# The low parts of the weights are written over the raw ones, panel loads wait for the end of a product, and x tiles are asked for ahead of the panel

## The reference

```
xn = rmsnorm(h, g_mix)
z, xbc, dt, q, k, v = split(xn @ w_in)               # w_in: 1024 x 2312
y_ssd = conv + SiLU + chunked state-space scan (8 heads x 64, state 128, chunks of 128)
y_att = sliding-window attention (8 heads, window 128, bias table, sinks)
h = h + concat(y_ssd, y_att) @ w_out                 # 1024 x 1024
h = h + cross_attention(rmsnorm(h), memory K/V)      # w_cq 1024 x 512, w_co 512 x 1024
h = h + (silu(hn @ w_gate) * (hn @ w_up)) @ w_down   # hn = rmsnorm(h); 1024 x 2816, 2816 x 1024
y = rmsnorm(h)
```

## Time and profile before

| | us |
|---|---|
| median of 3 runs | 3246.65 (3242.48 to 3249.24) |
| profiled execution, own time | 3245.05 |
| its span | 3243.3 |

### The profile page before, as it was taken

One profiled execution on the slowest core, in us unless ns is written; L12 is line 12 of the kernel. 1 busy time (PEld: TensorE's weight loads), 2 busy tenths in 40 slices (PEclk: granted clock), 3 DMA queues, 4 the chain that ended last, 5 costly groups with the idle time before them and its releaser, 6 DMA issues. The chain is left out here.

```text
span 3243.3 us, 35792 instructions
## 1 busy us (share of the span) xinstructions
PE 2996.9 (92%) x13972; PEld 2396.2 (74%) x13972; DVE 1484.3 (46%) x2221; ACT 1135.1 (35%) x1826; POOL 1027.3 (32%) x507
## 2 busy tenths in 40 slices
PE   7877999999999999999999999999779999667898
PEld 5656787877877878778778787788668888565742
DVE  5655655666346556553465566524352222313111
ACT  4542464345233543452346434422332222111100
POOL 3200433333444333334443333344224444410000
PEclk8988999999999999999999999999889999656679
DMA  4146423222335232223352222233313332571256
GB/s 132 53 116 155 136 72 89 71 72 79 98 107 166 72 88 72 72 79 97 107 167 78 85 72 66 85 97 114 107 40 97 98 98 91 152 210 45 64 183 222
DMA packets 490989, 332.44 MB, mean 103 GB/s; under 512 B 58559, under 2 KB 458051, under 8 KB 490806
## 3 DMA queue, kind: packets, MB, share of 16 engines
q1 hardware_dynamic: 486318, 323.74, 34.3%
q10 hardware_dynamic: 1880, 6.34, 0.5%
q0 software_dynamic: 2624, 0.09, 0.1%
HBM read 309.86 MB, written 21.23 MB: 102 GB/s over the span
## 5 line engine op out<-in xcount | busy, mean ns | idle before, releaser
L799 POOL TENSOR_TENSOR w_lo<-w_raw,w_hi 128x1024 fp32r<-128x1024 f32 x400 | 973.9, 2438 | 1717.6 <-ACT w_hi L813 1717.6
L1583 PE MATMUL L<-xa_h,w_hi 128*128 128x512 f32 x1536 | 613.2, 399 | 4.0 <-DVE xa_l L1402 4.0
L1584 PE MATMUL L<-xa_h,w_lo 128*128 128x512 f32 x1536 | 601.6, 392 | 0.0
L1585 PE MATMUL L<-xa_l,w_hi 128*128 128x512 f32 x1536 | 601.0, 391 | 0.0
L813 ACT ACTIVATE w_hi<-w_raw 128x1024 fp32r<-128x1024 f32 x400 | 421.1, 1053 | 437.6 <-PE L L1585 431.2
L1583 PEld LDWEIGHTS L<-xa_h,w_hi 128*128 128x128 f32 x1536 | 290.0, 189 | 75.1 <-issue 11.4
L1585 PEld LDWEIGHTS L<-xa_l,w_hi 128*128 128x128 f32 x1536 | 290.1, 189 | 61.6
L1584 PEld LDWEIGHTS L<-xa_h,w_lo 128*128 128x128 f32 x1536 | 290.4, 189 | 58.9 <-issue 1.0
L1542 DVE TENSOR_TENSOR sg<-sg,L 128x512 f32<-128x512 f32 x88 | 60.5, 688 | 531.4 <-PE L L1585 531.4
L1583 PE MATMUL L<-hid_h,w_hi 128*128 128x512 f32 x704 | 280.0, 398 | 6.1 <-DVE hT L1550 6.1
L1584 PE MATMUL L<-hid_h,w_lo 128*128 128x512 f32 x704 | 274.8, 390 | 0.0
(11 more groups left out here) (489 smaller groups left out, 4413.0 us busy)
## 6 DMA issues: line engine op xcount, KB each, us to landing
w_raw<-in_w_gate_dram SPq DMA_DIRECT2D x88, 512.0 KB, 3.8
w_raw<-in_w_up_dram SPq DMA_DIRECT2D x88, 512.0 KB, 3.8
w_raw<-in_w_down_dram SPq DMA_DIRECT2D x88, 512.0 KB, 3.4
w_raw<-in_w_in_dram SPq DMA_DIRECT2D x56, 512.0 KB, 3.8
xt<-xT_dram SPq DMA_DIRECT2D x48, 256.0 KB, 4.1
wS<-in_w_down_dram SPq DMA_DIRECT2D x11, 1024.0 KB, 4.9
wS<-in_w_gate_dram SPq DMA_DIRECT2D x10, 1024.0 KB, 5.1
wS<-in_w_up_dram SPq DMA_DIRECT2D x10, 1024.0 KB, 5.1
```

What stands on the lines that cost most here:

```text
L799: pool.tensor_tensor(w_lo[:, n % RING, 0:w], w_raw[:, n % RING, 0:w], w_hi[:, n % RING, 0:w].bitcast(F32), ALU.subtract)\
L1583: pe.matmul(acc, wh, rh, start=(k == 0), stop=False)
L1584: pe.matmul(acc, wl, rh, start=False, stop=False)
L1585: last = pe.matmul(acc, wh, rl, start=False, stop=(k == kn - 1))
```

## The change

- `w_lo` lies at the offset of `w_raw`: the subtraction writes its result over its own first input. The arena is 12288 bytes smaller, and all that lay behind the low parts moves down.
- Since the low part now lives in the raw place until its product has been made, `load_panel(n)` waits for `lin_out`, the end of product n-3, and no longer for its low part.
- x tiles: the first four of a block go ahead of panel w0+3, tile j four panels after the W step that uses tile j-4, and both tests are made before the panel's load (`x_before[t] <= n`), so that a tile is issued, and its wait stands, ahead of the load of that panel.
- In block 0 SP's transposition block stands at w0+3, as the waits of the other blocks do.

```diff
-            x_before.append(w0 + (5 if b == 0 else 4) if j < XR else min(w0 + use[j - XR][0] + 6, NPAN))
+            x_before.append(w0 + 3 if j < XR else min(w0 + use[j - XR][0] + 4, NPAN))
...
-        arena_bytes = 207232
+        arena_bytes = 207232 - 12288
...
-        O_H = 3 * RING * 4096
+        O_H = 2 * RING * 4096
...
-        w_lo = at("w_lo", O_LO, [P, RING, D], F32R)
+        w_lo = at("w_lo", O_RAW, [P, RING, D], F32R)
...
                 def load_panel(n):
                     if n >= RING:
-                        sp.wait_ge(s["lo_ready"], n - RING + 1)
+                        sp.wait_ge(s["lin_out"], first_out[n - RING + 1])
...
-                        if b == 0 and n == w0 + 4:
+                        if b == 0 and n == w0 + 3:
...
-                        if n == w0 + (4 if b == 0 else 3):
+                        if n == w0 + 3:
...
-                    load_panel(n)
-                    while t < len(x_tiles) and x_before[t] <= n + 1:
+                    while t < len(x_tiles) and x_before[t] <= n:
                         load_x_tile(t)
                         t += 1
+                    load_panel(n)
```

## The result

The changed kernel takes **3368.95 us**, median of 4 runs (3365.92 to 3373.53), against 3245.89 us of the kernel before beside it (4 runs): ratio 1.038, 95% interval 1.0362 to 1.0398. It is 123 us slower; 3335 was predicted, with a range of 3278 to 3385. The profiled execution took 3370.76 us, its span 3369.0 is 125.7 longer than the 3243.3 of before.

What follows compares the result with a forecast made beforehand. TensorE, busy 92% of the span, was taken as the bound. Terms 33.6 + 5.4 + 33.4 + 5.1 + 2.3 + 9 = 88.8 us on 3245.05 gave 3333.9, forecast as 3335; own range 3285 to 3378, 8 in 10 for 3278 to 3385.

Steps and rivals of the forecast that it cites:

- main case: Whole kernel: the listed costs sum to 88.8 us, giving 3335 us; chance 0.62.
- Down groups: First down panel of a group: ACT's landing wait and POOL delay hid_l and the eviction; 11 x 3.05 = 33.6 us.
- Groups with attention between products: The 9 other down groups in blocks 0 to 2: longer product slots cover part; 5.4 us.
- W: Output projection, blocks 1 to 3: y stores held behind SP's wait for a product, plus late x tiles; 33.4 us.
- Boundary: Block boundary, last down product: W's panel 1 lands later, squares wait, DVE recovers 1 us; 1.7 us three times, 5.1.
- W of block 0: Output projection of block 0, no y to store: high parts already at about T+5 behind ACT's own work; 0.
- K, Q and the input projection: K, Q and most of the input projection, all blocks: foretold at 0.
- O: Block 3's sums of squares before the O and Q ends meet a later POOL subtraction; 2.3 us.
- Clock: TensorE after idling may return at half rate: charged at a third of the 11 places and block 3's stall; 9 us.
- Hidden: Rival: weights keep 3.4 us of slack and landings are quick enough, so nothing changes, 3247 us; chance 0.06.
- Much slower: Rival: in attention stretches each pair of steps loses 1 to 1.3 us, some 18 pairs a block; 3390 us, chance 0.11.
- Faster: Rival: POOL's later subtraction frees DVE early in a product, and x tiles come early; some -12 us, 3235, chance 0.06.

Runs made afterwards that it cites:

- e2: Changed kernel with ACT making hid_h ahead of the next high part in a feed-forward step: 3306.36 us, 64 over the kernel before.
- e7: Kernel before with only the change's SP order (x tiles ahead of the panel, block 0's SP block a panel earlier): 3278.69 us, +34.
- e6: Kernel before with loads waiting for the end of the product three before, SP's block at block 0 a panel earlier: 3380.35 us, +138.
- e8: Changed kernel with four places in the ring instead of three: 3276.66 us, 32 over the kernel before.
- e9: e8 with the x tiles asked for behind the panel again, as late as in the kernel before: 3258.80 us, +17.
- e15: Kernel before with ACT's order alone: hid_h, and squares of outputs 0 and 1 of the last down group, ahead of the high part: 3245.05 us, +3.
- e3: Changed kernel with y chunks 0 and 1 stored ahead of load w0+6, and hid_h ahead of the next high part: 3287.71 us, +45.
- e5: e3 with block 1's row of norm factors loaded at chunk 7 of SP's block, not at its end: 3289.15 us, +45.
- e1: Changed kernel with y chunks 0 and 1 stored ahead of the load of W's panel w0+6: 3337.80 us, 95 over the kernel before.
- e4: e3 with squares of outputs 0 and 1 of the last down group made ahead of the next high part: 3272.76 us, +28.

## Why the prediction was right, and where it was not

The main case came: 123 us slower, 34 more than the sum, inside the range. The mechanisms were those foretold, and both large terms were right. That the whole lies in the range is in part luck: some 18 of the 34 us come from stretches that the sum had at 0, and the range reached so far for other reasons (a slow clock at every place, a dearer W).

- *Down groups.* 11 places at 3.05, 33.6 us. Measured, the 11 products come 2.92 to 3.76 us late, 33.6 in all, POOL's subtraction 0.47 us ahead of hid_l as in the earlier trace rows; e2 shows the cause.
- *Groups with attention between products.* 5.4 foretold, 6.9 measured, gone in e2.
- *W.* 33.4 against 32.6. The store goes 1.93 us after product w0+4 starts (1.95 foretold), but lands in 3.9 us (1010.01 to 1013.95), not 5.6 (which was given as the mean of 6.7 and 4.7; that is 5.7); that is made up by what follows, since products w0+6 and w0+7 come late too. What the sum did not have is that the x order would have made the store late by itself (e7); its 2 us for the x tiles was wrong in sign (e6).
- *Boundary, the term mis-sized:* 5.1, measured 12.9. I placed the late high part in the last product and let DVE recover. The one that costs is the product before: its first square waits behind the high part of W's first panel, DVE's copy behind that for POOL.
- *W of block 0, the step that failed:* 0, measured 5.9. The high part at about T+5 was taken to leave room for a later load and for x tiles ahead of it. Load w0+3, asked for at 321.50 and behind four x tiles, needed 11.7 us to land, the high part came at T+11.9 and TensorE idled 4.4 us. The x tiles ahead are not the whole of it, as e6 shows, where they stand behind: there that panel landed 5.7 us after its issue (320.01 to 325.69), but the first x tile, issued at 327.24, landed only at 330.7, ACT had its rounding ahead of the high part, and TensorE idled 4.7 us. With a load that waits for a product, one of the two is late. SP and ACT of the changed kernel, then DVE and ACT of e6:

```profile
321.50 3.89 SPq L662 DMA_DIRECT2D w_raw<-in_w_out_dram  x3
...
333.22 1.06 ACT L813 ACTIVATE w_hi<-w_raw 128x1024 fp32r<-128x1024 f32 x1 [4.81 <-DMA w_raw<-in_w_out_dram]
```

```profile
330.68 0.75 DVE L1131 SCALAR_TENSOR_TENSOR xt<-xt,pv,diag 128x512 f32<-128x512 f32 x1 [9.88 <-DMA xt<-xT_dram]
...
332.00 1.04 ACT L813 ACTIVATE w_hi<-w_raw 128x1024 fp32r<-128x1024 f32 x1
```

- *K, Q and the input projection, the largest miss:* 0, measured 12.1. TensorE's idle there grew by 5.6 us; the rest goes with the granted clock, 0.96 in blocks 1 and 2 where it was 0.97 and 1.00. With early loads (e7) or four places (e8, e9) the row is under 3; no experiment took it apart, so its cause stays open. *O:* 2.3, measured 5.8.
- *Clock, mis-sized:* 9, of which 6 at a third of the 11 places. Measured at 6 of the 11: the product behind the idle runs in part at 1.2 GHz and takes 7.0 to 8.5 us instead of 5.44, 13.7 us in all. The changed kernel in block 2 (busy by engine, granted clock, DMA share, GB/s), ahead of such an idle and behind it:

```profile
2186.00:2216.00 30.00, 30.00 (x134) 24.85 (x133) 7.30 (x6) 9.05 (x11) 12.37 (x6) 1.00 0.33 98
2219.30:2222.70 3.40, 3.40 (x8) 2.72 (x9) 0.43 (x1) 1.06 (x1) 1.48 (x1) 0.50 0.02 5
```

With the idle gone (e2) all of it came back: the rows are at 0.0. At the place of block 0 shown above, the same idle was followed by a product of nearly full speed (5.56 us); which places fall is not foretold by anything I found.

- *Rivals.* "Hidden" would have been right about the weights: e2 has the late landings and no stall in the feed-forward. "Much slower" did not come: its 18 pairs a block are the 6.9 us above. "Faster" had no trace.
- *POOL's hold on DVE.* In the sum it is priced for hid_l, which reads two SBUF tiles. That was half of it: a copy and a scaling with one tile as input are held too (L1142 2.15 us against 0.42 for the shortest; the scaling 2.60 in e15, L1411 there, against 0.47). The Trainium skill (SBUF — State Buffer, Practical consequences) names, beside two SBUF inputs, a two-port mode of VectorE that copies and `tensor_scalar` can enter; by that rule, the trace agrees. The held copy makes the boundary of the changed kernel, the held scaling (L1408, 2.59 us at 950.01) the 2.0 us of the kernel before.
- *The own range* was added up loosely: the named terms give some 3292 and 3376, not 3285 and 3378. Neither bears on the outcome.

## What to carry to other kernels

When a transfer is made later, look less at its own slack than at what stands behind the instruction that waits for it on each in-order engine: here 3.3 us later landings were harmless to the weights and cost 48 us through one rounding queued behind them, and that came back when the two changed places. A store or load that another engine waits for should not stand behind a wait for a product. Two edits can each be enough for the same stall; undoing one then shows too little, and doing each alone shows too much (22.6 and 47.5 us in W, 32.6 together).

## What the runs showed that I had not expected

The x order is good or bad by the loads' waiting: with early loads it costs 34 us, with late ones it saves some 15 (e6 against the change, in the medians and in W). From 316 to 322 us the DMA engines moved only 32 to 50 GB/s (0.62 to 0.96 busy in the changed kernel, e3 and e5), with and without the broadcast load, and the kernel before has this stretch too. x tiles landed in 11 to 15 us there, where the median of all is 3.4. A stretch that no edit touches can differ by some 4 us between two executions: up to W of block 0, e1, e3 and e4 have the same code and took 2.8, 0.6 and -1.0 us more than the kernel before. So nothing is argued here from a single stretch that moved by less.
